# Mixer sections of a two-block transformer kernel: where VectorE writes the remainders of the weight blocks, one RECIPROCAL in two halves, one high part earlier on ScalarE

## What is computed

```python
for l in range(DEPTH):                       # DEPTH = 2
    h = _rmsnorm(x, norm_mix[l])
    p_rw, p_sb, p_ret, p_conv = jnp.split(h @ w_in[l], MIX_SPLITS, axis=-1)
    branches = (rwkv7(p_rw), stick_breaking(p_sb), retention(p_ret), conformer_conv(p_conv))
    merged = sum(sigmoid(h @ w_gate[l, i]) * (branches[i] @ w_branch[l, i]))
    x = x + merged @ w_out[l]
    ...                                      # feed-forward part

# the start of rwkv7, where the edits lie
p = p + (_token_shift(p) - p) * mu           # the token shift
a = sigmoid(a0 + pa @ a2)
kk32 = k * k_k                               # per head
kk = kk32 / maximum(sqrt(sum(kk32 * kk32)), 1e-12)   # the key norm
k = k * (1.0 + (a - 1.0) * k_a)
```

## Time and profile before

| what | value |
|---|---|
| median of 3 runs | 1641.64 us (1641.52 to 1641.85) |
| the profiled execution | 1633.31 us, of which its span 1631.5 us |
| TensorE matmul busy | 1546.8 us, 95% of the span |
| VectorE busy | 1119.5 us, 69% |
| ScalarE busy | 810.5 us, 50% |
| mean granted TensorE clock | 0.976 |
| read from HBM | 290.22 MB |

### The profile page before, as it was taken

One profiled execution on the slowest core, in us unless ns is written; L12 is line 12 of the kernel. 1 busy time (PEld: TensorE's weight loads), 2 busy tenths in 40 slices (PEclk: granted clock), 3 DMA queues, 4 the chain that ended last, 5 costly groups with the idle time before them and its releaser, 6 DMA issues. The chain is left out here.

```text
span 1631.5 us, 24583 instructions
## 1 busy us (share of the span) xinstructions
PE 1546.8 (95%) x9902; PEld 1339.9 (82%) x9902; DVE 1119.5 (69%) x1642; ACT 810.5 (50%) x1083; POOL 18.4 (1%) x21
## 2 busy tenths in 40 slices
PE   8899989999999989998997899999999999978998
PEld 7789979899999978987986677777777779966677
DVE  5778864756555677886475788888888875257534
ACT  4643435354444464343533677777776744353422
POOL 1000000000000000000001000000000000000000
PEclk9999999999999999999999899999999998889999
DMA  8332222345556443222243399999999974412121
GB/s 315 132 127 91 91 91 91 122 163 183 192 181 194 161 143 117 91 91 91 91 156 121 126 342 351 345 339 335 346 358 340 341 260 159 139 65 78 65 92 64
DMA packets 82051, 292.95 MB, mean 180 GB/s; under 512 B 9095, under 2 KB 11647, under 8 KB 81679
## 3 DMA queue, kind: packets, MB, share of 16 engines
q1 hardware_dynamic: 81935, 291.34, 50.8%
HBM read 290.22 MB, written 1.08 MB: 179 GB/s over the span
## 5 line engine op out<-in xcount | busy, mean ns | idle before, releaser
L377 DVE TENSOR_TENSOR ring_lo<-ring,weights_hi 128x1024 fp32r<-128x1024 f32 x343 | 413.6, 1222 | 240.7 <-ACT weights_hi L356 238.0
L356 ACT ACTIVATE weights_hi<-ring 128x1024 fp32r<-128x1024 f32 x343 | 355.8, 1056 | 194.9 <-PE bank_P L272 158.4
L270 PE MATMUL bank_P<-h_hi,weights_hi 128*128 128x256 f32 x1456 | 427.9, 294 | 14.1 <-DVE ring_lo L377 8.5
L272 PE MATMUL bank_P<-h_hi,ring_lo 128*128 128x256 f32 x1456 | 414.6, 285 | 0.0
L271 PE MATMUL bank_P<-h_lo,weights_hi 128*128 128x256 f32 x1456 | 413.6, 284 | 0.0
L270 PEld LDWEIGHTS bank_P<-h_hi,weights_hi 128*128 128x128 f32 x1456 | 278.9, 192 | 24.7 <-issue 6.7
L272 PEld LDWEIGHTS bank_P<-h_hi,ring_lo 128*128 128x128 f32 x1456 | 283.0, 194 | 0.0
L271 PEld LDWEIGHTS bank_P<-h_lo,weights_hi 128*128 128x128 f32 x1456 | 279.1, 192 | 1.2 <-issue 0.5
L271 PE MATMUL bank_P<-ring_lo,gathered_hi 128*96 128x512 f32 (+1 forms) x384 | 144.0, 375 | 0.0
L377 DVE TENSOR_TENSOR ring_lo<-ring,tokens_hi 128x1024 fp32r<-128x1024 f32 x76 | 90.4, 1217 | 2.3 <-ACT tokens_hi L356 2.3
L377 DVE TENSOR_TENSOR ring_lo<-ring,tokens_lo 128x1024 fp32r<-128x1024 f32 x74 | 88.2, 1216 | 2.3 <-ACT tokens_lo L356 2.3
(11 more groups left out here) (501 smaller groups left out, 2718.5 us busy)
## 6 DMA issues: line engine op xcount, KB each, us to landing
ring<-stream SPq DMA_DIRECT2D x541, 512.0 KB, 4.5
cst<-consts SPq DMA_DIRECT2D x1, 1712.0 KB, 10.8
arena<-params SPq DMA_DIRECT2D x1, 1211.0 KB, 6.7
arena<-x SPq DMA_DIRECT2D x1, 1024.0 KB, 5.1
arena<-bias_vec SPq DMA_DIRECT2D x8, 128.0 KB, 2.9
out<-arena SPq DMA_DIRECT2D x2, 512.0 KB, 2.6
arena<-params SPq DMA_DIRECT2D x2, 256.0 KB, 7.7
arena<-bias_vec SPq DMA_DIRECT2D x8, 64.0 KB, 2.8
```

The costliest lines, as they stand in the source:

```text
L270: pe.matmul(out, hi, x_hi, start=start, stop=False, skip_group_check=True)
L272: return pe.matmul(out, lo, x_hi, start=False, stop=stop, skip_group_check=True)
L356: a.activation(self.slots[i % len(self.slots)], env["ring"][:, slot, :], ACT.Copy)\
L377: v.tensor_tensor(env["ring_lo"][:, slot, :], env["ring"][:, slot, :], self.slots[i % len(self.slots)].bitcast(F32), ALU.subtract).then_in ...
```

## The change

The same instructions run in another order on VectorE and ScalarE, with one RECIPROCAL of 128x512 as two of 128x256. The high and low parts, products and results are the same.

```diff
# ScalarE
+        hi.upto(15)
         a.wait_ge(*after("kk_ss"))
         act(kn, pair(BX), ACT.Sqrt, "kk_norm")
-        hi.upto(15)
+        hi.upto(16)
         a.wait_ge(*after("cum"))
         act(eP, cumL, ACT.Exp, scale=-RW_SCALE)
         act(eN, cumL, ACT.Exp, scale=RW_SCALE)
         act(eM, prev, ACT.Exp, "decays", scale=-RW_SCALE)
-        hi.upto(17)
+        hi.upto(18)
# VectorE
         for q in range(4):
-            lo.upto(2 * q + 4)
+            lo.upto((8, 9, 10, 11)[q])
             v.wait_ge(*after(f"rw_raw{q}"))
...
             ts(kp[:, j, :], av[:, j, :], 1.0, R("k_a", j), SUB, MUL)
+        lo.upto(15)
         stt(kp, kp, 1.0, pm[:, 2:4, :], ADD, MUL)
         v.wait_ge(*after("kk_norm"))
         for j in range(2):
             stt(scr[:, j, :], pm[:, j, :], R("r_k", j), kp[:, j, :], MUL, MUL, "rkr" if j else None)
-        lo.upto(15)
         ts(kn, kn, 1e-12, None, MAX)
-        link(v.reciprocal(kn, kn))
+        lo.upto(16)
+        for j in range(2):
+            link(v.reciprocal(kn[:, j, :], kn[:, j, :]))
+            lo.upto(17 + j)
         tt(kk, kk, kn, MUL)
         v.wait_ge(*after("decays"))
         lo.upto(17)
...
         for hh in range(4):
-            lo.upto(18 + hh)
+            lo.upto(19 + hh)
...
         for c4 in range(4):
-            lo.upto(22 + c4 // 2)
+            lo.upto(22 + (c4 + 1) // 2)
...
             tt(out, out, scr, ADD, name + "_in")
+            if name == "rot_q":
+                lo.upto(27)
         lo.upto(28)
```

## The result

| | before | after |
|---|---|---|
| runs | 1641.64 us, then 1641.58 us with one more | 1619.68 us median of 4 (1613.94 to 1621.12) |
| ratio, 95% interval | | 0.987 (0.9838 to 0.9902) |
| profiled execution | 1633.31 us, span 1631.5 | 1618.52 us, span 1616.7 |
| TensorE busy | 95% | 96% |
| mean granted clock | 0.976 | 0.974 |

By these runs the change makes the kernel 1.3% faster; over more executions, further on, it comes to 1.1 or 1.2%. The pair of profiled executions differs by 14.8 us, the pair of medians by 21.9. So there are two things to explain: whether the mixers did what was worked out, and why two ways of measuring one change differ by 7 us.

The account below looks back on a forecast made before the run. TensorE, 95% full, bounds the kernel. Waits of 8.7 and 9.0 us, less 0.8 a layer, plus 1.3 of clock in layer 0, give 17.4 off the median 1641.64: 1624.3, range 1621.5 to 1628.5 (forecast's own 1622.5 to 1626.5).

Parts of the forecast that it names:

- The bound and the six waits a layer: TensorE, 95% full, waits on VectorE's weight remainders at six blocks of each mixer: 8.7 us in layer 0, 9.0 in layer 1.
- The working block by block: Mixer blocks 8 to 26: start and end times carried along the new order; 0.8 us of waits stay in each layer.
- The halves of the RECIPROCAL: VectorE at the key norm: two halves cost 0.18 us more with the gap, but open a place 1.78 us earlier.
- The clock term: Block 15: with its wait cut to 0.3 us, 2.4 GHz expected, saving 1.3 us in layer 0, none in layer 1.
- 17.4: Total saving claimed in the two mixers: 9.2 us in layer 0 and 8.2 in layer 1.
- The rival by which the clock term would be absent: Timed runs lack layer 0's half-clock stretch at block 15: gain 16.1 us, time 1625.6; chance 0.18.
- the 8.3: Whole kernel before: the profiled execution, 1633.3 us, lay 8.3 below the runs' median; taken as not shown to depend on the mixers.

Follow-up runs that it names:

- x_whole: The changed kernel with one RECIPROCAL of 128x512 ahead of the remainders of blocks 16 and 17, instead of two halves; ratio to before 0.9868.
- x_act: The changed kernel with ScalarE's order of the high parts (blocks 14, 15, 17) put back as before; ratio to before 0.99.

## Why the prediction was right in its mechanism and wrong in its number

- **The bound and the six waits a layer: right.** Each part run alone took away its own waits and no other. The rest of the kernel moved up by them, but for what the clock takes or gives elsewhere (2.1 us between the mixers' starts in the first pair of traces).
- **The working block by block: right in the sum.** Remainders and high parts came within 0.25 us of the times listed; 0.8 us of waits a layer were to stay, and 1.1 and 0.9 us idle did. They were not spread as said: 0.23 at 15, 0.62 at 23 in place of 0.3, none at 24, and in layer 0 0.23 at block 5, which was not foreseen. The start of layer 0 became 9.3 us shorter (9.2 forecast), that of layer 1 8.5 (8.2), in the first pair of traces.
- **The halves of the RECIPROCAL: cost right (two of 1.74).** The prediction said that the split is no gain by itself and opens a place 1.78 us earlier; x_whole shows that this place is worth nothing either.
- **The clock term, 1.3 us in layer 0 and none in layer 1: mis-sized.** It was read from one trace. In the five traces with the wait of 2.65 us at block 15, the window around it is below 1.00 in 7 of 10 layers; in the eight traces without it, in 0 of 16. A start of before with the stretch is 1.4 us longer than one without in layer 0 (101.56, 100.15) and 1.6 in layer 1 (101.20, 99.65), so with 7 of 10 layers the term is about 2.1 us for the whole kernel (an estimate). The two kernels' starts, averaged over two traces of before (100.9 and 100.4 us) and three of after (92.0 and 91.2), differ by 8.9 and 9.2 us, 18.1 in all, against 17.4. The rival by which the clock term would be absent, 1625.6, pointed the wrong way: the stretch changes layer from trace to trace, but on average before paid more for it, not less. The Trainium skill ("TensorE: Matmul & The Clock Gate", Part 1) says that the gate's window runs free of the kernel. The traces agree in so far as one program has the stretch at block 15 in layer 0 in one execution and in layer 1 in another.
- **The step that failed: "Nothing in the rows says that the 8.3 depend on the mixers, so I take the same 17.4 from the median: 1641.64 - 17.4 = 1624.3".** The median of three executions of before was not its middle: the 67 taken later have a mean of 1637.8, and those three stood in the highest group. (1641.64 - 17.4 is 1624.2.) From the mean, the same sum gives 1620.4; the 15 executions of the changed kernel have a mean of 1619.1. So of the 5.2 us between the forecast and that mean, 3.8 come of the median of before. The 8.3 us between the profiled execution and the runs were a sign of that spread, and should have widened the range by some 4 us to either side. The prediction took this kernel to be told from itself to 3.3 us; single executions of it lie up to 10 us apart. The stated range allowed for unknown waits alone, and by its own terms (1.2 us more of waits in each layer, and 1 us) the forecast's own range would end at 1627.7, not 1626.5. With more executions the ratio came to 0.9892 and 0.9883; 17.4 of 1641.6 is 0.9894.

Of the remaining 1.3 us between 1620.4 and 1619.1, 0.7 is in the starts above; where the rest lies was not separated.

## What to carry to other kernels

Where one engine is full and the others only feed it, list its waits, add what a pipelined row hides (here 0.16 us each), and carry the new order through row by row: that gave times within 0.25 us. A feeding engine's order has to be moved on both stages of the feed: the new order of the remainders without the earlier high parts gave some 5 us less. Before taking a saving from a median, ask how far single executions of the kernel lie apart: a profiled execution 8 us off the runs was here no offset but the width of the distribution.

## What the runs showed that I had not expected

- One kernel's executions lie in separate groups, their means 2 to 7 us apart, ordered by their mean granted clock (0.974 on average in the lowest, 0.971 in the middle, 0.969 in the highest of before). Some of the stretches that come and go, as that at 1538 us, stand behind idle time on TensorE (1.42 us there) and far from any edit. That the groups come from such stretches is shown for one pair of traces, from the lowest and the middle group; for the rest only the order of the mean clocks speaks.
- A wait of 2.65 us behind a block of 2.9 us that itself followed a wait of 1.42 was followed by a stretch at 1.2 GHz in 7 of 10 cases; one wait of 1.32 alone (x_act, two layers) was not.
- A short half-clock stretch cost 1.5 to 1.7 us on products with no wait behind them (near 217, 600 and 645 us in the second trace of before), and next to nothing at 211 us in the first, where TensorE waited soon after anyway.
